# Hybrid attention step: one slot per step of a head, indexer scores in two blocks, the whole search under the projection

## The chip, the cores and the metric

The kernel runs on one core of a Trainium2 chip. A core has TensorE (PE: matrix products, its results go to the PSUM banks), VectorE (DVE), ScalarE (ACT), GpSimd (POOL) and SyncE (SP), which here only issues DMAs. Each engine runs its own instructions in the order of the program; semaphores tie the engines together. The metric is the time of one execution on the device in microseconds, lower is better.

## What is computed

One encoder layer for 1024 prompt tokens and 64 tokens of a second request that has 256 cached keys. All is float32. Cut to what matters:

```
h = rms_norm(x) * (1 + scale) + shift                      # modulated by silu(c) @ w_ada
dq,dk,dv, sq,sk,sv, iq,ik,iw = split(h @ w_in)             # 4 differential heads, 8 sparse heads, 4 indexer heads
# differential head:
a = softmax(q1 k1 + bias) - lam * softmax(q2 k2 + bias)    # keys up to the query's chunk of 64
o = rms_norm(a @ v, g_subln) * (1 - lam_init)
# sparse heads: the indexer picks min(256, L // 4) keys for each query
score = sum_h w[h] * relu(q_idx[h] . k_idx)
keep  = top_k(score)
o = softmax(q k + bias, over the kept keys) @ v
x = x + gate1 * rms_norm(concat(o) @ w_out)
x = x + gate2 * rms_norm(swiglu(h2) @ w_down)
```

The rows of dk, dv, sk, sv and ik are outputs too.

## The kernel before

The tokens form nine tiles t: eight of 128 prompt tokens, tile 8 the 64 others. Tile t sees n = 128(t+1) keys, tile 8 sees 320. The program has five parts: the modulation, the input projection in 21 blocks of 128 columns and three chunks of rows each, the attention, the output projection, and the FFN in eleven groups.

**Projection and search.** `chunk(b, c)` (L1775) makes one chunk as 24 products in three-term split precision. Between the chunks of blocks 3 to 6 stand the indexer's products, `dots(t, p)` (L1779, rows L1791): tiles 2 to 8, two heads at a time into both S banks, 14 pairs in all. ACT applies relu (L1119), DVE adds the weighted heads into `work` (L1442, L1446). A pair waits until ACT has read the pair before it. `dots_tiles` gives two tiles to each of blocks 3, 4 and 5 and tile 8 to block 6. Then DVE searches for each row's threshold: `STEPS` = 33 passes, in each of which it counts the scores above a candidate in all seven tiles (L1379) and then updates the candidates (L1397 to L1431). 28 passes run one after another beside the projection (`PROJ_STEPS`). The five others are dealt out over the first 13 slots of the attention (`LATE_PARTS`). After the passes that stand under the projection DVE makes the gates (L1460 to L1471), and PE waits for these (`gates_ready`) before it begins the attention.

**Attention.** Eight steps s for each tile, 72 in all: i = 0 to 3 are the differential heads ("dense" here, with two score maps m = 0, 1), i = 4 to 7 pairs of sparse heads (m is the head). Each engine runs a loop over slots; what an engine does in slot k belongs to several steps:

- PE, in this order: turns the first half of the weights of step k-2 (transposes, L1856), score products of step k into the banks S[0] and S[1] (L1881, plus the mask for sparse steps, L1887), turns the other half, turns the output of step k-3 (L1935), value products of step k-2 into the bank PJ[0] (L1956, L1959).
- DVE: adds the bias to map 0 of step k (L1558, which also gives the maximum), takes the reciprocals of the sums of step k-1 (L1499, L1501) and combines its two maps (L1567) or scales map 0 (L1575), adds the bias to map 1 (L1558), scales map 1 of a sparse step, reads the products of step k-2 (L1588, L1593).
- ACT: copies turned weights from the two T banks to `aT` (L1134), exponentials of step k (L1224).
- POOL: the rms of a dense head (L831, L834).
- SP: refills a ring of four bias tiles `ering` (`load_e`, L704, two DMAs for each); entry e waits until the bias of entry e-4 was added. It also loads the queries and values of the tile after next.

A dense step has one group of turned weights (8 transposes at 1024 keys), a sparse step two. The scores of step k wait until both maps of step k-1 have been read (`biased`).

At three slots near the start of each tile from 2 to 8 the ties at the threshold are settled: `compare` (DVE, slot 8t-2), turning the equal marks (PE, L1898, slot 8t-1), `ranks` (PE, L1916, into PJ[1]) and `choose` (DVE, L1525, L1529) for keys 0 to 511 in slot 8t and for the others in slot 8t+1.

Once all value products up to tile 7 are done SP loads w_out (`owraw`, L751), one block between every two bias tiles of tile 8; the output projection (L1978) starts when tile 0's split outputs are ready.

## Time and profile before

| what | us |
| --- | --- |
| median of 3 runs | 1673.65 (1671.73 to 1674.25) |
| the profiled execution | 1676.04 |
| its span in the trace | 1674.0 |
| projection, end of PE's last chunk | 382 |
| first bias of the attention | 388.5 |
| first bias of tile 2 | 459.0 |
| first bias of tile 8 | 706.1 |
| first product of the output projection | 752.0 |

The profile page gives the busy time of each engine, the span in 40 slices with TensorE's granted clock, and the chain of work that ended last. Besides, the trace answers what ran on an engine in a stretch (the timeline: start, duration, engine, line, what it wrote and read, count, and in brackets the idle time just before it with the engine that ended it), and how long each engine was busy in a stretch, with the clock granted there (1.00 is 2.4 GHz, 0.50 is 1.2 GHz). Busy times of PE count matmuls that overlap, so that a busy PE need not be one at its peak.

### The profile page before, as it was taken

Reading aid. Unit: us, or ns where it says so; the run is one execution under the profiler, and the core shown is the slowest. Engines: PE = TensorE matmul, PEld = TensorE weight load, DVE = VectorE, ACT = ScalarE, POOL = GpSimd, SP = SyncE. Lnnn points to the kernel's source line nnn. Section 1 sums busy time; section 2 is a strip of 40 time slices with the busy share of each in tenths; the row PEclk is TensorE's granted clock in tenths of the full one; section 3 lists DMA queues with packets and bytes.
Section 4 is the critical chain, followed back from the end, with each engine's and each line's share of the span. In section 5 each row is a group of like instructions: output and inputs, shape, how many; then the busy total and the mean of one; then the engine's idle time right before and its main releaser. Section 6 shows DMA issues by size and latency. Waiting matters only on the chain.

```text
span 1674.0 us, 24041 instructions
## 1 busy us (share of the span) xinstructions
PE 1535.3 (92%) x9123; PEld 1317.8 (79%) x9123; DVE 761.0 (45%) x1766; ACT 541.7 (32%) x1101; POOL 407.8 (24%) x361
## 2 busy tenths in 40 slices
PE   5999999994678889879999999999999999999996
PEld 3776998993345566648879999999999999999994
DVE  4423999996877777653430321303122031221305
ACT  4345222212466666662542112121121221112102
POOL 3010111111001000054546231332313222232315
PEclk8899999996599999969999999999999999999998
DMA  9210465522244444341442110111011021110006
GB/s 300 79 45 26 129 213 183 179 90 80 68 119 123 125 128 124 84 153 40 125 131 83 51 51 25 50 50 50 25 50 50 25 69 31 50 50 25 0 1 125
DMA packets 147336, 142.49 MB, mean 85 GB/s; under 512 B 11982, under 2 KB 129039, under 8 KB 147259
## 3 DMA queue, kind: packets, MB, share of 16 engines
q1 hardware_dynamic: 146026, 137.01, 27.9%
q0 software_dynamic: 1232, 4.46, 1.5%
q8 instruction: 48, 0.79, 0.2%
q14 instruction: 30, 0.24, 0.1%
HBM read 122.14 MB, written 19.29 MB: 84 GB/s over the span
## 4 chain that ended last, share of the span: by engine, by line
PE 82%; DVE 8%; issue 3%; ACT 3%; POOL 2%; DMA 1%; SPq 1%; DVEq 0%; POOLq 0%; ACTq 0%
PE S L2017 31%; PE PJ L1746 14%; PE T L2040 10%; PE PJ L2040 5%; PE S L1881 4%; DVE sc L1558 3%; PE S L1978 3%; PE PJ L1978 3%; PE T L1856 3%; PE PJ L1956 2%; PE S L1709 1%; DVE scrap L1379 1%; PE S L1791 1%; PE S L1887 1%; ACT aT L1134 1%
## 5 line engine op out<-in xcount | busy, mean ns | idle before, releaser
L2017 PE MATMUL S<-h2h,gh 128*128 128x352 f32 (+1 forms) x1056 | 347.9, 329 | 7.5 <-POOL gl L895 4.0
L2017 PE MATMUL S<-h2h,gl 128*128 128x352 f32 (+1 forms) x1056 | 346.7, 328 | 0.0
L2017 PE MATMUL S<-h2l,gh 128*128 128x352 f32 (+1 forms) x1056 | 346.5, 328 | 0.0
L1664 DVE TENSOR_TENSOR hv<-sg,S 128x352 f32<-128x352 f32 (+1 forms) x66 | 35.1, 532 | 490.1 <-ACT sg L1278 478.0
L2017 PEld LDWEIGHTS S<-h2h,gh 128*128 128x128 f32 x1056 | 199.6, 189 | 8.4 <-issue 7.9
L2017 PEld LDWEIGHTS S<-h2l,gh 128*128 128x128 f32 x1056 | 200.4, 190 | 0.4
L2017 PEld LDWEIGHTS S<-h2h,gl 128*128 128x128 f32 x1056 | 199.3, 189 | 0.0
L1379 DVE TENSOR_SCALAR_CACHE_REDUCE scrap<-work,cand 128x384 uint8<-128x384 f32 (+6 forms) x217 | 180.1, 884 | 1.1
L2040 PE MATMUL T<-dh,ahl 128*128 128x512 f32 x504 | 166.5, 390 | 0.0
L1746 PE MATMUL PJ<-hTh,wh 128*128 128x352 f32 (+2 forms) x480 | 161.3, 336 | 0.0
L1278 ACT ACTIVATE sg<-S 128x352 f32<-128x352 f32 (+1 forms) x66 | 31.2, 474 | 399.6 <-PE S L2017 399.6
L1746 PE MATMUL PJ<-hTl,wh 128*128 128x352 f32 (+2 forms) x480 | 158.4, 330 | 0.0
L1746 PE MATMUL PJ<-hTh,wl 128*128 128x352 f32 (+2 forms) x480 | 158.4, 330 | 0.0
L922 POOL TENSOR_TENSOR ahl<-hv,ahl 128x352 fp32r<-128x352 f32 (+1 forms) x66 | 61.0, 925 | 354.9 <-ACT ahl L1134 354.9
L1224 ACT ACTIVATE sc<-sc,nmax 128x128 f32<-128x128 f32 (+8 forms) x144 | 107.8, 749 | 84.1 <-DVE nmax L1558 83.1
L1558 DVE CUSTOM_DVE_ANT_0 sc<-S,ering 128x128 f32<-128x128 f32 (+8 forms) x144 | 104.2, 724 | 47.5 <-PE S L1881 31.1
L1671 DVE TENSOR_TENSOR yacc<-yacc,T 128x512 f32<-128x512 f32 x132 | 90.7, 688 | 75.2 <-PE T L2040 75.2
L840 POOL TENSOR_TENSOR wl<-wraw,wh 128x1024 fp32r<-128x1024 f32 (+1 forms) x21 | 49.6, 2364 | 287.6 <-ACT wh L976 287.6
L2040 PEld LDWEIGHTS T<-dh,ahl 128*128 128x128 f32 x504 | 94.6, 188 | 20.2 <-DVE yacc L1671 0.8
L1856 PE MATMUL T<-ident,sc 128*128 128x128 f32 (+2 forms) x468 | 76.7, 294 | 30.3 <-DVE sc L1567 21.1
L2040 PE MATMUL T<-dl,ahl 128*128 128x512 f32 x264 | 102.9, 390 | 0.0
L895 POOL TENSOR_TENSOR gl<-graw,gh 128x2048 fp32r<-128x2048 f32 x22 | 101.2, 4602 | 2.0 <-ACT gh L1134 2.0
(244 smaller groups left out, 2466.4 us busy)
## 6 DMA issues: line engine op xcount, KB each, us to landing
graw<-in_w_gu SPq DMA_DIRECT2D x44, 512.0 KB, 5.0
ada<-in_w_ada SPq DMA_DIRECT2D x16, 1024.0 KB, 7.4
draw<-in_w_down SPq DMA_DIRECT2D x22, 512.0 KB, 3.3
wraw<-in_w_in SPq DMA_DIRECT2D x20, 512.0 KB, 5.6
ada_first<-in_w_ada SPq DMA_DIRECT2D x8, 1024.0 KB, 12.5
q_scratch<-qst SPq DMA_DIRECT2D x8, 544.0 KB, 2.9
xin<-in_x_p SPq DMA_DIRECT2D x8, 512.0 KB, 7.0
owraw<-in_w_out SPq DMA_DIRECT2D x8, 512.0 KB, 4.9
```

The lines of the kernel that those rows point to most:

```text
L895: pool.tensor_tensor(gl[slot][:, :, :], graw[slot][:, :, :], gh[slot][:, :, :].bitcast(F32), ALU.subtract).then_inc(g_lo, 1)
L922: last = pool.tensor_tensor(al[:, slot, c0:c0 + p], hv[:, u % 2, 0:p], ah[:, slot, c0:c0 + p].bitcast(F32), ALU.subtract)
L1224: nc.scalar.activation(p, p, ACT.Exp, scale=-1.0, bias=nmax[0:r, slot % 4, m:m + 1], accum_out=rsum[0:r, slot % 4, m:m + 1]).then_inc(exp_ ...
L1379: ins = nc.vector.tensor_scalar(out, work[0:r, o:o + n], least_score, None, ALU.is_ge, ALU.add, accum_out=rows_at(count, i))
L1558: nc.vector.tensor_tensor_reduce(out=sc[0:r, s % 3, m, 0:n], in0=S[m][0:r, 0:n], in1=rev, scale=-1.0, scalar=3.0e38, op0=ALU.add, op1=ALU.min,
L1671: nc.vector.tensor_tensor(at, at, YB[u % 3][:, :], ALU.add).then_inc(y_added, 1)
L1746: last = pe.matmul(chunk_bank(3 * b + c)[0:w, 0:n], wp[:, b % 2, k, 0:w], hp[:, k, c0:c0 + n], start=(k == 0 and p == 0), stop=(k == KB - ...
L1856: last = pe.transpose(bank[0:w, 128 * j:128 * j + r], sc[0:r, s % 3, m, o:o + w], ident[0:r, 0:r])
L1881: last = pe.matmul(S[m][0:r, o:o + w], qt[part, t % 2, i, 0:r], keys, start=True, stop=not kept)
L1978: last = pe.matmul(OUT[t % 2][0:r, cols_], op[:, k, 0:r], wp[:, k, cols_], start=(k == 0 and p == 0), stop=(k == KB - 1 and p == 2))
L2017: last = pe.matmul(S[u % 2][:, 512 * part:512 * part + n], wp[slot][:, k, 128 * part:128 * part + 128], hp[:, k, c0:c0 + n], start=(k == 0 ...
L2040: last = pe.matmul(YB[u % 3][:, :], ap, wp[:, b, 512 * half:512 * half + 512], start=(b == 0 and p == 0), stop=(b == 1 and p == len(parts) ...
```

## The change

Four things change, all of them in order and buffers; no operation is added or left out.

1. `dots_pairs` puts the eight pairs of tiles 2 to 5 into block 3 and the six of tiles 6 to 8 into block 4: one before each chunk and one in the middle of each; what is left of a block's pairs follows its last chunk.
2. All 33 search passes run before the gates. `LATE_PARTS`, `late_parts` and `scrap2` go.
3. In the attention the step that an engine works on in slot k is k-1 for the exponentials, k-2 for combining or scaling (DVE), k-3 for turning the weights (PE, ACT), k-4 for the value products, k-5 for the last scaling of a dense head, and k-6 for turning its output. There are 78 slots where there were 75. `sc` gets a fourth buffer (`sc_last`), `aT` a second, and the value products use PJ[0] and PJ[1] in turn; `ranks` takes the one that the value products don't use in that slot.
4. The order within a slot becomes, on PE: value products, all transposes of weights, equal marks, output, scores, ranks; on DVE: both biases, combining or scaling, last scaling, reading of the products, compare, choose.

Two waits come with it: the value products wait until `choose` has read its bank in the slot before (`rank_read`), and `ranks` waits until the products of the step before have been read (`wait_products_read`).

PE in a slot of tile 7 with a dense step (T<-ident,sc are the transposes of weights, S<-kTp,qt the scores, T<-ident,ob the output of a head, PJ the value products). Before:

```order
L1959 MATMUL PJ<-vsbp,aT 128x128 [waits o_read,ld_v1,t_freed1,t_freed0]
L1959 MATMUL PJ<-vsbp,aT 128x128 x7
L1856 MATMUL T<-ident,sc 128x128 [waits t_freed0,combined]
L1856 MATMUL T<-ident,sc 128x128 x3
L1856 MATMUL T<-ident,sc 128x128 [waits t_freed1,combined]
L1856 MATMUL T<-ident,sc 128x128 x3
L1881 MATMUL S<-kTp,qt 128x512 [waits biased]
L1881 MATMUL S<-kTp,qt 128x512 x3
```

Now, the last dense slot of the tile:

```order
L1958 MATMUL PJ<-aT_107,vsbp 64x128 [waits t_freed1,t_freed0,pair_read]
L1958 MATMUL PJ<-aT_107,vsbp 64x128 x13
L1871 MATMUL T<-ident,sc 128x128 [waits t_freed0,combined]
L1871 MATMUL T<-ident,sc 128x128 x3
L1871 MATMUL T<-ident,sc 128x128 [waits t_freed1,combined]
L1871 MATMUL T<-ident,sc 128x128 x3
L1896 MATMUL S<-kTp,qt 128x512 [waits biased]
L1896 MATMUL S<-kTp,qt 128x512 x3
```

Read as a ring the order of these three is the same, but the weights that are turned ahead of the scores of step k were those of step k-2 and are those of step k-3. For a sparse step the second half of the transposes stood behind the scores, and now all of them stand ahead.

DVE in a dense slot of the same tile (ISA sc,nmax<-S,ering is the bias, L1567 and L1571 combine the maps). Before:

```order
L1499 RECIPROCAL rinv<-rsum 128x2 [waits exp_done]
L1501 SCALAR_TENSOR_TENSOR rlam<-rinv,lam,rsum 128x1 [waits vchain]
L1567 SCALAR_TENSOR_TENSOR sc<-sc,rlam 128x1024 [waits vchain]
L1558 ISA sc,nmax<-S,ering 128x1024 [waits ld_e3,qk_done]
L1558 ISA nmax 128x1
```

Now (the row ISA sc,nmax comes twice, with a row of its accumulator behind each):

```order
L1557 ISA sc,nmax<-S,ering 128x1024 [waits t_filled0,t_filled1,ld_e0,qk_done]
L1557 ISA nmax 128x1
L1557 ISA sc,nmax<-S,ering 128x1024 [waits ld_e1,qk_done]
L1557 ISA nmax 128x1
L1508 RECIPROCAL rinv<-rsum 128x2 [waits exp_done]
L1510 SCALAR_TENSOR_TENSOR rlam<-rinv,lam,rsum 128x1 [waits vchain]
L1571 SCALAR_TENSOR_TENSOR sc<-sc,rlam 128x1024 [waits vchain]
```

The bias of map 1 stood behind the combining and stands ahead of it now.

PE at the second slot of tile 7, where the ranks of ties are made (PJ<-upto,eqT). Before:

```order
L1956 MATMUL PJ<-aT,vsbp 64x128 [waits t_freed1,t_freed0,o_read]
L1956 MATMUL PJ<-aT,vsbp 64x128 x13
L1916 MATMUL PJ<-upto,eqT 128x512 [waits rank_read]
L1916 MATMUL PJ<-upto,eqT 128x512 x4
L1916 MATMUL PJ<-upto,eqT 128x384
L1916 MATMUL PJ<-upto,eqT 128x256
L1916 MATMUL PJ<-upto,eqT 128x128
L1856 MATMUL T<-ident,sc 128x128 [waits t_freed0,combined]
L1856 MATMUL T<-ident,sc 128x128 x3
L1856 MATMUL T<-ident,sc 128x128 [waits t_freed1,combined]
```

Now:

```order
L1931 MATMUL PJ<-upto,eqT 128x384
L1931 MATMUL PJ<-upto,eqT 128x256
L1931 MATMUL PJ<-upto,eqT 128x128
L1958 MATMUL PJ<-aT_89,vsbp 64x128 [waits t_freed0,pair_read,t_freed1,rank_read]
L1958 MATMUL PJ<-aT_89,vsbp 64x128 x13
L1871 MATMUL T<-ident,sc_last 128x128 [waits t_freed0,scaled]
L1871 MATMUL T<-ident,sc_last 128x128 x3
L1871 MATMUL T<-ident,sc_last 128x128 [waits t_freed1,scaled]
L1871 MATMUL T<-ident,sc_last 128x128 x2
L1871 MATMUL T<-ident,sc_last 128x128 [waits t_freed0,scaled]
```

The value products (PJ<-aT) follow the ranks across the slot's border and have got a wait for `rank_read`, and the transposes behind them wait with them.

The diff, cut to its core:

```diff
-PROJ_STEPS = 28
-LATE_PARTS = [(j, i) for j in range(PROJ_STEPS, STEPS) for i in range(len(TOPK_TILES) + 1)]
-LATE_POINTS = 3 * 13
-def dots_tiles(b):
-    return [t for t in TOPK_TILES if b == 3 + (t - 2) // 2]
+def dots_pairs(b, point):
+    pairs = [(t, p) for t in {3: [2, 3, 4, 5], 4: [6, 7, 8]}.get(b, []) for p in range(2)]
+    return pairs[point:point + 1] if point < 6 else pairs[6:]
...
+SCALE_LAG, TURN_LAG, VALUE_LAG, OUT_LAG = 2, 3, 4, 6
+SLOTS = NSTEPS + OUT_LAG
...
+        sc_last = place("sc_last", [128, 2, 1024], F32, 183296)
+        aT.append(then("aT1", [128, 2, 8, 128]))
...
             dve.wait_ge(targets_set, 3 * len(TOPK_TILES) + 1)
-            for j in range(PROJ_STEPS):
+            for j in range(STEPS):
...
             for slot in range(SLOTS):
                 for m in range(2):
                     if slot < NSTEPS:
+                        biases(slot, m)
+                s = behind(slot, SCALE_LAG)
+                if s is not None:
+                    weights(s)
+                s = behind(slot, VALUE_LAG + 1)
+                if s is not None and not sparse(s):
+                    head_scaled(s)
+                s = behind(slot, VALUE_LAG)
+                if s is not None and not sparse(s):
+                    head_read(s)
                 if tie_stage(slot, 0):
                     compare(tie_stage(slot, 0))
                 for q in range(2):
                     t = tie_stage(slot, 2 + q)
                     if t and 512 * q < nkeys(t):
-                        choose(t, q)
+                        choose(t, q, PJ[(slot + 1) % 2])
...
-            def chunk(b, c):
+            def chunk(b, c, between):
...
                 for k in range(KB):
+                    if k == KB // 2:
+                        for pair in between:
+                            dots(*pair)
                     chunk_rows(b, c, k)
...
+            def value_products(s):
...
+                for q in range(2):
+                    u = tie_stage(s + VALUE_LAG - 1, 2 + q)
+                    if u and 512 * q < nkeys(u):
+                        pe.wait_ge(rank_read, rank_count(u, q))
...
             for slot in range(SLOTS):
-                for key in prob_part(slot, 0):
-                    transpose_probs(key)
-                if slot < NSTEPS:
-                    scores(slot)
-                for key in prob_part(slot, 1):
-                    transpose_probs(key)
+                s = behind(slot, VALUE_LAG)
+                if s is not None:
+                    value_products(s)
+                s = behind(slot, TURN_LAG)
+                if s is not None:
+                    for key in prob_groups(s):
+                        transpose_probs(key)
                 if tie_stage(slot, 1):
                     turn_equals(tie_stage(slot, 1))
...
+                if slot < NSTEPS:
+                    scores(slot)
                 for q in range(2):
                     t = tie_stage(slot, 2 + q)
                     if t and 512 * q < nkeys(t):
-                        ranks(t, q)
+                        if slot > VALUE_LAG:
+                            wait_products_read(pe, slot - VALUE_LAG - 1)
+                        ranks(t, q, PJ[(slot + 1) % 2])
```

## Rows read from the trace of the kernel before

**Rows 1.** Busy times by stretch: start:end us, length, each engine, clock, DMA share, GB/s

```profile
388.50:459.00 70.50, 39.91 (x165) 22.20 (x167) 61.87 (x238) 25.95 (x101) 5.94 (x16) 0.53 0.31 76
459.00:706.10 247.10, 213.96 (x1627) 138.92 (x1626) 183.06 (x482) 156.80 (x367) 17.82 (x48) 1.00 0.43 119
...
652.30:667.16 14.86, 12.97 (x114) 8.56 (x114) 10.58 (x18) 9.09 (x18) 0.00 (x0) 1.00 0.41 96
667.16:692.50 25.34, 22.73 (x142) 14.98 (x143) 19.14 (x44) 14.91 (x27) 2.97 (x8) 1.00 0.39 113
692.50:706.10 13.60, 12.38 (x119) 8.72 (x118) 9.03 (x19) 9.92 (x21) 0.00 (x0) 1.00 0.18 39
706.10:752.00 45.90, 33.75 (x239) 20.00 (x239) 26.22 (x84) 28.23 (x82) 20.36 (x16) 0.67 0.45 142
```

**Rows 2.** Waits of PE from 459.0 to 706.1: us, times, longest

```profile
PE T L1856 <- DVE sc L1567: 13.8, 21, 1.1
```

**Rows 3.** Timeline of PE in tile 7: start us, us, engine, line, out<-in

```profile
670.12 1.09 PE L1856 MATMUL T<-ident,sc 128*128 128x128 f32 x8 [0.99 <-DVE sc L1567]
671.26 1.99 PE L1881 MATMUL S<-kTp,qt 64*128 64x512 f32 x8
673.18 0.33 PE L1935 MATMUL T<-ident,ob 128*128 128x128 f32 x1
673.55 2.02 PE L1959 MATMUL PJ<-vsbp,aT 128*128 128x128 f32 x16
676.22 1.09 PE L1856 MATMUL T<-ident,sc 128*128 128x128 f32 x8 [0.65 <-DVE sc L1567]
```

**Rows 4.** Timeline of DVE over the same slot, and a sparse scaling

```profile
673.28 1.23 DVE L1558 CUSTOM_DVE_ANT_0 sc<-S,ering 128x1024 f32<-128x1024 f32 x1 [0.24 <-PE S L1881]
...
674.43 0.16 DVE L1499 RECIPROCAL rinv<-rsum 128x2 f32<-128x2 f32 x1
674.62 0.22 DVE L1501 SCALAR_TENSOR_TENSOR rlam<-rinv,lam,rsum 128x1 f32<-128x1 f32 x1
674.88 1.28 DVE L1567 SCALAR_TENSOR_TENSOR sc<-sc,rlam 128x1024 f32<-128x1024 f32 x1
676.08 1.22 DVE L1558 CUSTOM_DVE_ANT_0 sc<-S,ering 128x1024 f32<-128x1024 f32 x1
...
688.00 0.75 DVE L1575 TENSOR_SCALAR sc<-sc,rinv 128x1024 f32<-128x1024 f32 x1
```

**Rows 5.** Timelines of PE and DVE in the first slot of tile 7

```profile
654.14 1.75 PE L1956 MATMUL PJ<-aT,vsbp 128*64 128x128 f32 x28 [0.94 <-ACT aT L1134]
...
656.58 0.75 DVE L1525 SCALAR_TENSOR_TENSOR eq<-PJ,need,eq 128x512 bf16<-128x512 f32 x1 [0.49 <-PE PJ L1916]
```

**Rows 6.** Timeline of the projection: two products 10 apart; the search's ends, a slow step

```profile
169.85 0.32 PE L1746 MATMUL PJ<-hTh,wl 128*128 128x352 f32 x1
171.46 0.32 PE L1746 MATMUL PJ<-hTh,wh 128*128 128x352 f32 x1
...
174.51 0.55 DVE L1379 TENSOR_SCALAR_CACHE_REDUCE scrap<-work 128x384 uint8<-128x384 f32 x1
...
304.83 2.38 POOL L840 TENSOR_TENSOR wl<-wraw,wh 128x1024 fp32r<-128x1024 f32 x1 [12.38 <-ACT wh L976]
304.88 2.35 DVE L1423 TENSOR_TENSOR good<-count,target 128x7 f32<-128x7 f32 x1
...
375.70 0.17 DVE L1428 TENSOR_SCALAR step<-step 128x7 f32<-128x7 f32 x1
```

**Rows 7.** Timelines of SP's queue and DVE: second round of bias tiles, step 4's bias

```profile
396.93 15.60 SPq L704 DMA_DIRECT2D ering<-r_scratch  x14
...
405.57 0.28 DVE L1558 CUSTOM_DVE_ANT_0 sc<-S,ering 128x128 f32<-128x128 f32 x1
```

**Rows 8.** Busy times by stretch, the columns as in rows 1

```profile
718.00:721.40 3.40, 1.85 (x12) 0.97 (x12) 2.36 (x11) 1.54 (x8) 0.73 (x2) 1.00 0.73 231
721.40:724.80 3.40, 3.40 (x14) 1.27 (x12) 2.20 (x8) 2.33 (x7) 1.46 (x3) 0.50 0.76 225
```

More of the change, by code:

```diff
@@ L142, in prob_groups, with behind @@
     return [("p", s, m, q) for m in range(2 if sparse(s) else 1) for q in range((n + 3) // 4)]
[L145 to L150 removed]
+def behind(slot, lag):
+    return slot - lag if lag <= slot < NSTEPS + lag else None
 def tie_stage(slot, lag):
@@ L184 @@
 T_ORDER += [("gates",)]
-for _s in range(NSTEPS + 3):
-    if 2 <= _s < NSTEPS + 2:
-        T_ORDER += prob_groups(_s - 2)
+for _s in range(SLOTS):
+    if behind(_s, TURN_LAG) is not None:
+        T_ORDER += prob_groups(_s - TURN_LAG)
     if tie_stage(_s, 1):
         T_ORDER += eq_groups(tie_stage(_s, 1))
-    if _s >= 3 and not sparse(_s - 3):
-        T_ORDER += [("o", _s - 3)]
+    if behind(_s, OUT_LAG) is not None and not sparse(_s - OUT_LAG):
+        T_ORDER += [("o", _s - OUT_LAG)]
 T_ORDER += [("f", t, half) for t in range(NT) for half in range(2)]
@@ L1109, in _ @@
             for b in range(NB):
-                pairs = [(t, p) for t in dots_tiles(b) for p in range(2)]
                 for c in range(4):
-                    for t, p in pairs[c:c + 1]:
+                    for t, p in dots_pairs(b, 2 * c) + dots_pairs(b, 2 * c + 1) if c < 3 else dots_pairs(b, 6):
                         r, n = rows_of(t), nkeys(t)
@@ L1208, in _ @@
             for slot in range(SLOTS):
-                if 3 <= slot < NSTEPS + 3 and sparse(slot - 3):
-                    pair_out(slot - 3)
-                for part in range(2):
-                    for key in prob_part(slot, part):
+                s = behind(slot, VALUE_LAG)
+                if s is not None and sparse(s):
+                    pair_out(s)
+                s = behind(slot, TURN_LAG)
+                if s is not None:
+                    for key in prob_groups(s):
                         prob_out(*key[1:])
@@ new lines, in weights @@
+            def weights(s):
+                _, _, r, n = step(s)
+                sums(s)
+                if sparse(s):
+                    for m in range(2):
+                        p = probs(s, m)[0:r, 0:n]
+                        nc.vector.tensor_scalar(p, p, rinv[0:r, s % 4, m:m + 1], None, ALU.mult
+                                                ).then_inc(scaled, 1)
+                else:
+                    nc.vector.scalar_tensor_tensor(out=probs(s, 0)[0:r, 0:n], in0=probs(s, 1)[0:r, 0:n],
+                                                   scalar=rlam[0:r, s % 4:s % 4 + 1], in1=probs(s, 0)[0:r, 0:n],
+                                                   op0=ALU.mult, op1=ALU.subtract).then_inc(combined, 1)
@@ L1561, in _ @@
-                    if m == 0 and 1 <= slot <= NSTEPS:
-                        sums(slot - 1)
-                    if m == 0 and 1 <= slot <= NSTEPS and not sparse(slot - 1):
-                        s = slot - 1
-                        _, _, r, n = step(s)
-                        nc.vector.scalar_tensor_tensor(out=sc[0:r, s % 3, 0, 0:n], in0=sc[0:r, s % 3, 1, 0:n],
-                                                       scalar=rlam[0:r, s % 4:s % 4 + 1], in1=sc[0:r, s % 3, 0, 0:n],
-                                                       op0=ALU.mult, op1=ALU.subtract).then_inc(combined, 1)
@@ L1597, in _ @@
-                for part in late_parts(slot, 2):
-                    search_part(*part)
+                        biases(slot, m)
[3 more added lines that the diff above has]
+                s = behind(slot, VALUE_LAG + 1)
+                if s is not None and not sparse(s):
+                    head_scaled(s)
+                s = behind(slot, VALUE_LAG)
+                if s is not None and not sparse(s):
+                    head_read(s)
@@ L1815, in _ @@
                     pe.wait_ge(chunk_out, 9)
-                pairs = [(t, p) for t in dots_tiles(b) for p in range(2)]
                 for c in range(4):
-                    for pair in pairs[c:c + 1]:
+                    for pair in dots_pairs(b, 2 * c):
                         dots(*pair)
                     if c < 3 and (b, c) not in FIRST_CHUNKS:
-                        chunk(b, c)
+                        chunk(b, c, dots_pairs(b, 2 * c + 1))
                     if c < 3 and b == 2:
@@ L1927, in _ @@
+            for slot in range(SLOTS):
+                s = behind(slot, VALUE_LAG)
+                if s is not None:
+                    value_products(s)
+                s = behind(slot, TURN_LAG)
+                if s is not None:
+                    for key in prob_groups(s):
+                        transpose_probs(key)
                 if tie_stage(slot, 1):
                     turn_equals(tie_stage(slot, 1))
-                if 3 <= slot < NSTEPS + 3 and not sparse(slot - 3):
-                    s = slot - 3
-                    r = rows_of(s // 8)
+                s = behind(slot, OUT_LAG)
+                if s is not None and not sparse(s):
+                    r = step(s)[2]
```

197 lines of the change are left out of this document (90 added, 107 removed).

## The prediction

> **What bounds the kernel now.** I read the page's 40 slices first, then the busy times by stretch, then the waits and timelines inside one tile. From 459.0 to 706.1 us (tiles 2 to 7) PE is busy 213.96 of 247.10 us at a granted clock of 1.00, DVE 183 [rows 1]: PE bounds these tiles, with 33.1 us of gaps. The largest named wait is that of the turned weights for DVE's combining, 13.8 us in 21 waits [rows 2]. The first two tiles are different: 70.5 us, PE busy 39.9 at clock 0.53, DVE 61.9, so that DVE with the late search and the supply of bias tiles set their time [rows 1]. The last 45.9 us (tile 8 and the drain) run at 0.67 [rows 1].
>
> The dense slot of tile 7 shows how the engines depend on each other. Scores start at 671.26, map 0's bias at 673.28 (2.02 later), the reciprocal 1.15 after that, then 0.19, 0.26 and 1.20 to the end of combining; the transposes start 0.14 later at 676.22, and take 1.14 up to the next scores [rows 3, 4]. The sum is 6.10 us, the slot's length (670.12 to 676.22) [rows 3]. So a dense slot is already one closed loop PE, DVE, PE, and only the bias of map 0 stands in it; map 1's bias runs beside the transposes.
>
> **The change part by part. 1, attention of tiles 2 to 7.** The larger distance between steps would open the loop if PE gave DVE the scores early. But PE still issues the scores of step k behind the transposes, now those of step k-3; DVE makes these weights in slot k-1, behind both biases of step k-1, and these need the scores of step k-1. So the loop closes over one slot again: scores, bias 0, bias 1, combining, transposes, scores. It contains all it had plus map 1's bias, 1.15: 6.10 + 1.15 = 7.25 us. Value products (2.02) don't add to it; PE has them while DVE works.
> - Slots 3 to 6 of tile 7 on PE: 7.25; with the mask products of a sparse step 7.9 twice (a slot with them takes 0.64 more now); with mask and output turning (0.37, rows 3) 8.2. Sum 31.25 instead of 25.34 [rows 1]: +5.9.
> - Slots 1 and 2, with ties. Here the value products at the head wait for `choose`, which is the last thing on DVE, and everything else of PE is queued behind them: transposes, scores, ranks; DVE waits for those scores in its turn. 2.02 (scores), 2 x 1.15 (biases), 0.2 (sums), 2 x 0.67 (scalings, row of 0.75 less overlap), 0.79 (`choose`), 1.75 (value products), 2.0 (both halves of the transposes) make 10.4, with an output 10.8 [rows 3 to 5]; with 0.4 for handovers 21.6 for both instead of 14.86 [rows 1]: +6.7. The second operation of `choose` frees no bank and is left out.
> - Slot 7 and slot 0 of the next tile: sparse scalings instead of combining, both halves of transposes, output, equal marks: 9.5 and 7.0, the latter with tile 8's small scores. 16.5 instead of 13.60 [rows 1]: +2.9.
>
> Tile 7: +15.5. If this falls with the keys (384 to 1024 in tiles 2 to 7, together 4.125 times tile 7's), it is 64 us for the six tiles; if it doesn't fall, 93. I take **+70**, near the lower end, since most terms are by element, but handovers aren't.
>
> **2, TensorE's clock.** Now PE is busy 0.87 of the time in tiles 2 to 7 and keeps 1.00 [rows 1]. In the tie slots it would idle some 5 us in one piece, in dense slots 7.25 - 5.2 = 2 us. In the tail the clock read 1.00 over 718.0 to 721.4, where PE was busy 1.85 of 3.40, and 0.50 (1.2 GHz) right after, with PE busy all the time [rows 8]. Such a stretch at half rate loses 1.7 us, two of them 3.4: I take 2.5 for a fall, and one fall at each of the 11 tie slots of tiles 2 to 8: **+28**. Bounds: 0 (no fall) and 45 (falls outside the tie slots too). The Trainium skill, "TensorE: Matmul & The Clock Gate", section "HAM oscillation", describes the same pattern: short bursts of matmuls with waits between them put the array back to half rate every time. By that rule the 28 stands, without it the sum is 28 lower.
>
> **3, first two tiles.** Five search passes leave DVE: 35 counts and 5 updates, at the projection's 7.2 us a pass (201.4 us from 174.51 to 375.87 for 28, rows 6) 33 to 36 us of its 61.9. Not all of this is won. Slots 0 to 3 use bias tiles that are loaded; SP issues the next only at 396.93, behind its loads of values [rows 7], which the change doesn't move, so step 4 can't start before about 400.6, by my estimate of landing (it starts at 405.57 now, rows 7): 4.9 won. The other twelve slots take 4.46 us each now; with two biases, combining and copies at 128 and 256 keys and PE at half clock I estimate 3.3: 14 won. Together **-19**, bounds -10 (each slot still bound by bias tile supply or PE at clock 0.53) and -30 (all of DVE's relief).
>
> **4, projection.** The 14 pairs stay, twice as dense: one every half chunk. Ten products take 1.61 us [rows 6], half a chunk (12) 1.9; a pair has to wait for ACT's two relus, about 2 us, so PE waits little inside the chunks, but three pairs stand back to back at the end of block 3. I take **+4**, 0 to 9 with a clock fall. The dots end 4.5 chunks (of 24 products, 3.9 us) earlier, with the turns of natural rows some 21 us: the search begins near 153.5. 33 passes at 7.2 end at 391, 9 us past the projection's end of 382 and 15 later than the passes now. Costed at about nothing: before 388.5 no bias starts today, and step 4 is held to 400.6 by SP anyway; without that cover it would cost 3 to 8. One row bears on the pass's length: an update's two-input operation took 2.35 us where it met POOL's subtraction of 2.38 [rows 6], while its like take 0.17. The Trainium skill, "SBUF - State Buffer", section "Who interferes with whom", has it so: an operation of VectorE with two inputs in SBUF can't run while GpSimd reads SBUF through the shared pair. The 7.2 contains these meetings, and the five added passes would meet one or two more.
>
> **5, tail.** Three more slots, and SP's wait for the last value products stands behind all bias issues. 45.9 us now [rows 1]. Each drain slot costs a turn of transposes, copies and products, about 3: **+9**, bounds 4 and 14.
>
> Costed at nothing: exponentials a slot later (ACT has 34 us of work in tile 7's 53.8, rows 1), POOL's rms, the fourth `sc` and second `aT` (no operation more), `ranks`' wait for products read a slot before. Added DMAs: none. Out-projection and FFN unchanged.
>
> **Sum.** The profiled execution took 1676.0, 2.4 over the median. 1676.0 + 70 + 28 - 19 + 4 + 9 = 1768; less 2.4 gives **1765 us**, 5.5% more.
>
> **The rivals.**
> - *A, loop without clock falls.* PE idles, but the clock stays at 1.00. For it: in 459 to 706 it never fell, though single waits of 1 us stood there; against it: rows 8. 1765 - 28 = 1737, 1718 to 1745.
> - *B, faster: the pipeline opens.* If DVE has the weights of step k-3 combined before PE reaches the transposes, PE's waits go. That is so if biases, sums and combining (2 x 1.15 + 0.45 + 1.20 = 3.95) are done while PE still has work behind the scores. For it: the step distance is one more, and PE's work for a dense slot is only 5.2. Against it: after the scores PE has only value products, 2.02, from which 3.95 decides against; it would turn at a combining under 2 us. All gaps gone: 1673.7 - 19 - 33 = 1622, about 1624 with rests.
> - *C, a smaller loop.* DVE starts bias 0 while map 1's scores still run, and value products cover more: half of the 70, no falls, and a cheap tail: 1690 to 1715.
> - *D, the change doesn't do what it says.* The search isn't all under the projection: it ends after 391, with more meetings, and the cover of part 4 is too short. +8: 1773.
>
> **How the numbers follow.** Forecast (loop and falls, 1745 to 1795) 0.52; A 0.30; B 0.08; C 0.05; D 0.03; within the measurement's reach 0.02. What a measurement of this kernel can tell from no change is about 0.2%. Faster by more than that: B, 0.08. Within: 0.02. Slower: the rest, 0.90. The range must take in A and most of C: from 1712; above, the upper ends of the loop (93 instead of 70) and clock (45 instead of 28) don't both come: 1800. Left out are B, some of C and a little above 1800.
>
> **What would show it.** The dots ending and the search beginning near 153; search ending near 388 to 391, with PE's gates right behind; first bias about 391; tile 2's at 440 to 446. In tile 7 dense slots of 7.3 to 8 us, in them PE's first transposes waiting some 2 us for the combining, and the second bias standing ahead of it; tie slots of 10 to 11 us in which the value products wait for `keep` or `eq` of DVE. Granted clock under 1.00 in slices of tiles 2 to 7 (if 1.00 stays: A). PE's waits for DVE in tiles 2 to 7 over 80 us instead of 13.8. The prediction is wrong if dense slots stay at or under 6.1, or if tiles 2 to 7 together take under 290 us.

## The result, and the profile after

The changed kernel takes 1766.09 us, median of four runs (1762.67 to 1774.72), against 1673.95 for the kernel before: the ratio is 1.056 (95% interval 1.052 to 1.060). The profiled execution took 1766.25 us, with a span of 1764.4. The times of stages that follow are those of one profiled execution each, taken at the same marks in every kernel: PE's last chunk of the projection, the first bias of a tile, the first product of the output projection, the end.

| stage | before, us | after, us | difference | forecast |
| --- | --- | --- | --- | --- |
| start to the end of the projection | 381.8 | 380.0 | -1.8 | +4 |
| to the first bias | 6.7 | 6.7 | 0.0 | 0 |
| tiles 0 and 1 | 70.5 | 55.9 | -14.6 | -19 |
| tiles 2 to 7 | 247.1 | 346.1 | +99.0 | +98 |
| tile 8 and drain, to the output projection | 45.9 | 54.3 | +8.4 | +9 |
| output projection and FFN | 922.0 | 921.4 | -0.6 | 0 |
| sum | 1674.0 | 1764.4 | +90.4 | +92 |

Nearly all of the loss is in one stage, tiles 2 to 7. (Its forecast is the +70 for the loop and the whole +28 for the clock; one of the 11 falls behind the 28, 2.5 us, belongs to tile 8's stage.) The busy times of the attention's three stretches after the change (start:end, length, each engine, granted clock, DMA share, GB/s; they answer to [rows 1]):

```profile
386.66:442.60 55.94, 39.77 (x151) 22.14 (x152) 27.18 (x143) 24.43 (x97) 6.20 (x16) 0.50 0.39 100
442.60:788.70 346.10, 245.38 (x1599) 155.61 (x1598) 180.55 (x482) 154.34 (x364) 21.33 (x48) 0.89 0.31 84
788.70:842.97 54.27, 33.39 (x281) 22.87 (x281) 29.16 (x88) 31.70 (x90) 20.28 (x16) 0.75 0.36 119
```

In tiles 2 to 7 PE's gaps have grown from 33 to 101 us, DVE's busy time is about the same (180.6 against 183.1), and the clock is 0.89 where it was 1.00. PE's busy time is 31 us longer, since a product lasts longer at the lower clock: with the clock held at 0.98 (`pe_kept_busy` below) PE is busy 210 us with the same work. PE's waits in that stretch (us in total, times, longest) say for whom; they answer to [rows 2], where the first group was 13.8 us and DVE's `eq` did not appear:

```profile
PE PJ L1958 <- DVE eq L1534: 30.3, 10, 4.2
PE T L1871 <- DVE sc L1571: 29.5, 18, 2.4
PE T L1871 <- DVE sc_last L1571: 9.5, 6, 1.9
PE T L1871 <- DVE sc L1568: 9.4, 10, 1.1
```

The first is the value products behind `choose`, the next two are transposes behind the combining of a dense step, the last is transposes behind a sparse scaling. Together they are 78.7 us, and with the smaller groups behind them, for equal marks (2.8) and one more sparse scaling (1.7), PE waits 83 us for DVE.

One dense slot of tile 7, on PE and then on DVE, answers to [rows 3] and [rows 4]. L1557 is the bias, L1571 combines, L1871 are the transposes, L1896 the scores:

```profile
737.88 1.75 PE L1958 MATMUL PJ<-aT,vsbp 128*64 128x128 f32 x28
742.07 1.09 PE L1871 MATMUL T<-ident,sc 128*128 128x128 f32 x8 [2.44 <-DVE sc L1571]
743.09 1.99 PE L1896 MATMUL S<-kTp,qt 64*128 64x512 f32 x8
745.01 2.05 PE L1961 MATMUL PJ<-vsbp,aT 128*128 128x128 f32 x16
749.19 1.09 PE L1871 MATMUL T<-ident,sc 128*128 128x128 f32 x8 [2.13 <-DVE sc L1571]
```

```profile
737.98 1.22 DVE L1557 CUSTOM_DVE_ANT_0 sc<-S,ering 128x1024 f32<-128x1024 f32 x1 [5.44 <-PE S L1896]
739.13 0.08 DVE L1557 DVE_READ_ACCUMULATOR2_ANT nmax<- 128x1 f32 x1
739.13 1.22 DVE L1557 CUSTOM_DVE_ANT_0 sc<-S,ering 128x1024 f32<-128x1024 f32 x1
...
740.27 0.16 DVE L1508 RECIPROCAL rinv<-rsum 128x2 f32<-128x2 f32 x1
740.47 0.22 DVE L1510 SCALAR_TENSOR_TENSOR rlam<-rinv,lam,rsum 128x1 f32<-128x1 f32 x1
740.73 1.29 DVE L1571 SCALAR_TENSOR_TENSOR sc<-sc,rlam 128x1024 f32<-128x1024 f32 x1
745.11 1.22 DVE L1557 CUSTOM_DVE_ANT_0 sc_last<-S,ering 128x1024 f32<-128x1024 f32 x1 [3.10 <-PE S L1896]
```

Read it as a ring. The scores end about 737.9, both biases take 2.3, sums and combining 1.75, the transposes start at 742.07, the scores at 743.09, and the next bias at 745.11. The slot is 7.13 us; it was 6.10. DVE idles 3.10 us for PE's scores, and PE idles 2.44 for DVE's combining: each waits for the other within one slot, and no engine is full.

A slot with ties, PE and DVE:

```profile
718.64 3.25 PE L1958 MATMUL PJ<-aT,vsbp 128*64 128x128 f32 x28 [4.15 <-DVE eq L1534]
721.83 1.65 PE L1871 MATMUL T<-ident,sc 128*128 128x128 f32 x7
...
731.96 1.75 PE L1958 MATMUL PJ<-aT,vsbp 128*64 128x128 f32 x28 [3.10 <-DVE eq L1534]
```

```profile
713.87 1.22 DVE L1557 CUSTOM_DVE_ANT_0 sc<-S,ering 128x1024 f32<-128x1024 f32 x1 [3.76 <-PE S L1896]
...
716.36 1.28 DVE L1568 TENSOR_SCALAR sc<-sc,rinv 128x896 f32<-128x896 f32 x2
717.56 0.28 DVE L1596 TENSOR_SCALAR ob<-ob,oss 128x128 f32<-128x128 f32 x1
717.75 0.75 DVE L1534 SCALAR_TENSOR_TENSOR eq<-PJ,need,eq 128x512 bf16<-128x512 f32 x1
```

DVE has had the scores since 713.87, but works through two biases, two scalings and a head's last scaling before `choose` reads the ranks; only then may PE's value products, transposes and scores go on. This slot took 13.5 us, the next 10.6. The first of them ran at the lower clock: the same 28 products took 3.25 us, 1.75 in the next slot. The clock around it, by stretch:

```profile
713.00:716.40 3.40, 1.49 (x8) 0.32 (x6) 2.49 (x6) 1.37 (x4) 0.00 (x0) 1.00 0.00 0
716.40:719.80 3.40, 1.16 (x12) 1.19 (x14) 2.79 (x5) 0.00 (x0) 0.00 (x0) 0.50 0.65 168
719.80:723.20 3.40, 3.40 (x27) 3.05 (x23) 0.00 (x0) 0.50 (x2) 0.00 (x0) 0.50 0.39 66
```

PE was busy for 1.49 us of the stretch, then the clock is 0.50 (1.2 GHz), and it is still so while PE works all the time again. In the next slot PE waited 3.10 us for `choose`, and the clock stayed at 1.00: the 28 products behind that wait took 1.75 us.

### The profile page after: what moved, and what is told of

Same layout as the page of the kernel before. It is cut to its first block, busy times and chain, and to the rows that moved or that the text cites. A ratio compares the mean times of both kernels' runs of the same rounds, so it can differ in the third digit from the quotient of the medians.

```text
span 1764.4 us, 24048 instructions
## 1 busy us (share of the span) xinstructions
PE 1564.3 (89%) x9123; PEld 1336.5 (76%) x9123; DVE 754.6 (43%) x1766; ACT 541.3 (31%) x1101; POOL 410.8 (23%) x361
## 4 chain that ended last, share of the span: by engine, by line
PE 79%; DVE 9%; issue 4%; ACT 4%; DMA 2%; SPq 1%; POOL 1%; POOLq 0%; DVEq 0%; ACTq 0%
PE S L2040 30%; PE PJ L1759 13%; PE T L2063 10%; PE S L1896 5%; PE PJ L2063 5%; PE T L1871 3%; PE S L2001 3%; PE PJ L2001 2%; DVE sc L1557 2%; PE PJ L1958 2%; DVE sc L1568 1%; PE S L1722 1%; ACT aT L1140 1%; DVE sc L1571 1%; PE S L1807 1%
## 5 line engine op out<-in xcount | busy, mean ns | idle before, releaser
L1557 DVE CUSTOM_DVE_ANT_0 sc<-S,ering 128x128 f32<-128x128 f32 (+8 forms) x108 | 74.7, 725 | 166.2 <-PE S L1896 103.6
L1871 PE MATMUL T<-ident,sc 128*128 128x128 f32 (+1 forms) x351 | 59.4, 308 | 64.4 <-DVE sc L1571 41.6
L847 POOL TENSOR_TENSOR wl<-wraw,wh 128x1024 fp32r<-128x1024 f32 (+1 forms) x21 | 49.5, 2356 | 286.2 <-ACT wh L983 286.2
L1140 ACT ACTIVATE aT<-T 128x512 f32<-128x512 f32 (+4 forms) x168 | 68.9, 453 | 151.4 <-PE T L1871 151.1
L838 POOL TENSOR_SCALAR oss<-oss 128x1 f32<-128x1 f32 (+1 forms) x36 | 8.5, 236 | 408.0 <-DVE oss L1587 408.0
L1871 PEld LDWEIGHTS T<-ident,sc 128*128 128x128 f32 (+1 forms) x351 | 41.7, 155 | 81.3 <-DVE sc L1571 48.0
```

What stands on the lines that cost most here:

```text
L847: pool.tensor_tensor(wl[:, b % 2, :, 0:n], wraw[:, b % 2, :, 0:n], wh[:, b % 2, :, 0:n].bitcast(F32), ALU.subtract).then_inc(w_lo, 1)
L1140: act_copy = lambda out, in_, **kw: nc.scalar.activation(out, in_, ACT.Copy, **kw)
L1557: nc.vector.tensor_tensor_reduce(out=probs(s, m)[0:r, 0:n], in0=S[m][0:r, 0:n], in1=rev, scale=-1.0, scalar=3.0e38, op0=ALU.add, op1=ALU.m ...
L1871: last = pe.transpose(bank[0:w, 128 * j:128 * j + r], probs(s, m)[0:r, o:o + w], ident[0:r, 0:r])
```

## The experiments

All times are medians, and ratios are to the kernel before. The stages, in us, come from each kernel's own trace; the last column runs from tile 8's first bias. The diffs are cut to their core, and "..." marks what is left out.

| kernel | us | ratio (95%) | tiles 0, 1 | tiles 2 to 7 | clock there | to the output projection |
| --- | --- | --- | --- | --- | --- | --- |
| before | 1673.95 | | 70.5 | 247.1 | 1.00 | 45.9 |
| changed | 1766.09 | 1.052 to 1.060 | 55.9 | 346.1 | 0.89 | 54.3 |
| before_search | 1654.66 | 0.987 to 0.991 | 49.5 | 247.1 | 1.00 | 45.9 |
| before_search_only | 1673.46 | 0.996 to 1.000 | 47.0 | 247.1 | 1.00 | 45.9 |
| weights_mid | 1732.23 | 1.032 to 1.038 | 51.6 | 313.8 | 0.92 | 54.8 |
| choose_early | 1752.08 | 1.041 to 1.049 | 55.6 | 334.4 | 0.89 | 51.5 |
| pe_kept_busy | 1748.25 | 1.042 to 1.045 | 55.8 | 325.0 | 0.98 | 56.0 |
| scores_first | 1633.88 | 0.974 to 0.977 | 44.2 | 223.4 | 1.00 | 54.7 |
| first_mid | 1663.32 | 0.992 to 0.996 | 47.0 | 249.9 | 1.00 | 55.4 |
| first_choose | 1636.54 | 0.974 to 0.980 | 44.9 | 227.7 | 0.99 | 55.7 |
| before_first_both | 1660.30 | 0.989 to 0.994 | 50.5 | 254.0 | 0.99 | 47.9 |
| halves_apart | 1625.78 | 0.967 to 0.973 | 45.1 | 211.1 | 1.00 | 58.3 |

**Is it the attention or the search?** `before_search` has only the first half of the change (parts 1 and 2 of its list).

```diff
-PROJ_STEPS = 28
+PROJ_STEPS = STEPS
...
-    return [t for t in TOPK_TILES if b == 3 + (t - 2) // 2]
+    pairs = [(t, p) for t in {3: [2, 3, 4, 5], 4: [6, 7, 8]}.get(b, []) for p in range(2)]
+    return pairs[point:point + 1] if point < 6 else pairs[6:]
...
```

> The kernel before with the first half of the change alone: indexer pairs in blocks 3 and 4, all 33 passes under the projection, attention order as before. My budget of the change has -16 us for this half (tiles 0 and 1 14.6 shorter, projection unchanged within 1), and all of the loss from the attention's order: 1655 to 1662. Rival, tiles 0 and 1 gain from the attention's order (more distance between steps) and not from DVE's relief: 1668 or more.

1654.66 us, 19 under the kernel before, at the lower edge of the expected band. Tiles 2 to 7 are at 247.1 to the tenth, so the whole loss of the change comes from its second half. Tiles 0 and 1 take 49.5 us here and 55.9 in the changed kernel: the new attention order costs 6.4 us even there.

```profile
385.80:435.30 49.50, 38.17 (x165) 21.45 (x167) 28.27 (x147) 25.46 (x101) 5.92 (x16) 0.56 0.46 108
435.30:682.40 247.10, 214.00 (x1627) 138.96 (x1628) 183.14 (x482) 156.72 (x367) 17.72 (x48) 1.00 0.44 119
```

**Do the denser indexer pairs matter?** `before_search_only` moves the passes, but leaves the pairs in blocks 3 to 6.

```diff
-PROJ_STEPS = 28
+PROJ_STEPS = STEPS
```

> The kernel before with all 33 passes ahead of the gates, and the indexer's pairs left in blocks 3 to 6. In before_search (pairs in blocks 3 and 4 as well) the search ran from 147.0 to 379.0, the projection ended at 379.1 and the first bias came at 385.8. Here the search begins near 172 to 174, so that it ends near 404 to 406, the first bias comes near 411 to 413, 20 us or more after the projection, and tiles 0 and 1 take about 50: the whole is 1672 to 1682, the gain of moving the passes used up. Rival: PE's start is not held by the gates so long, since bias tiles are late in any case: 1660 to 1668.

1673.46 us, no difference from before that a measurement can tell. The search ran from 172.9 to 407.9, and PE waited 29.0 us for the gates. Tiles 0 and 1 gain 23.4 us, but the first bias comes at 410.3 instead of 388.5. So the earlier pairs are what makes the moved passes worth something: 19 us.

```profile
PE T L1844 <- DVE lam L1471: 29.0, 1, 29.0
```

**Is the place of the scores the cause?** `scores_first` moves one call to the head of PE's slot. The weights' transposes and the value products of a slot now come behind its scores.

```diff
             for slot in range(SLOTS):
+                if slot < NSTEPS:
+                    scores(slot)
                 s = behind(slot, VALUE_LAG)
...
-                if slot < NSTEPS:
-                    scores(slot)
```

> The changed kernel with one move: PE issues the scores of a slot at its head, ahead of value products and transposes. My theory (the loop closes over one slot because the scores stand behind the transposes, which wait for DVE's combining behind both biases): the loop opens. PE's work of a dense slot of tile 7 is 2.0 + 2.0 + 1.1, so dense slots fall from 7.1 to 9.3 to 5.2 to 5.9 us, PE's waits for DVE nearly vanish, the granted clock is 1.00 in tiles 2 to 7, these take 225 to 245 us (346 in the changed kernel, 247 before), and the whole 1635 to 1660 us, faster than before. Rival 1, the loop is real but the wait of the value products for choose is the larger half: tiles 2 to 7 stay over 290, the whole over 1705. Rival 2, the greater distance itself costs (longer chains through ACT and the T banks): nothing or little comes back, over 1740.

1633.88 us, 1 under the expected band: 132 us less than the changed kernel by this one move, and 40 less than the kernel before. Tiles 2 to 7 take 223.4 us, the clock is 1.00, and dense slots of tile 7 take 5.92, 5.16, 5.55 and 5.54. Both rivals fall: the greater distance is no cost of itself, and the wait for `choose` goes with the loop (0.16 us in the last row below, a slot at the start of tile 8). PE has hardly a gap; the largest that are left are those for ACT's copies:

```profile
432.70:656.10 223.40, 202.04 (x1562) 134.71 (x1557) 181.00 (x483) 150.95 (x362) 21.34 (x48) 1.00 0.49 132
```

```profile
PE T L1982 <- ACT aT L1140: 7.4, 16, 0.7
PE T L1871 <- ACT aT L1140: 5.4, 10, 0.7
```

```profile
662.31 1.97 PE L1958 MATMUL PJ<-aT,vsbp 128*64 128x128 f32 x32 [0.16 <-DVE eq L1534]
```

**What is map 1's bias worth in the loop?** `weights_mid` leaves PE as in the changed kernel, and puts the combining back between the biases.

```diff
-                for m in range(2):
-                    if slot < NSTEPS:
-                        biases(slot, m)
+                if slot < NSTEPS:
+                    biases(slot, 0)
                 s = behind(slot, SCALE_LAG)
                 if s is not None:
                     weights(s)
+                if slot < NSTEPS:
+                    biases(slot, 1)
```

> The changed kernel with DVE's order as before: bias of map 0, combining or scaling, bias of map 1. My theory has map 1's bias as 1.15 us of the dense loop of tile 7 and nothing of the sparse one beyond that: dense slots of tile 7 fall from 7.1 to 7.7 to 6.0 to 6.6, tiles 2 to 7 from 346 to about 310, the whole to 1720 to 1740. If only the wait for choose and the clock matter, it stays over 1755. If the loop were the whole story, tiles 2 to 7 would return to 247 and the whole to about 1665.

1732.23 us, within the expectation, with tiles 2 to 7 at 313.8. The four dense slots of tile 7 are 6.10, 6.74, 6.64 and 7.17 instead of 7.13, 9.32, 7.67 and 9.94; the first three are the lengths of the kernel before to a hundredth of a microsecond. The wait for the combining halves, and the wait for `choose` stays:

```profile
PE PJ L1959 <- DVE eq L1534: 30.0, 10, 4.2
PE T L1872 <- DVE sc L1571: 16.8, 18, 1.3
```

**What does `choose` cost at the end of DVE's slot?** `choose_early` moves it behind the biases.

```diff
+                for q in range(2):
+                    t = tie_stage(slot, 2 + q)
+                    if t and 512 * q < nkeys(t):
+                        choose(t, q, PJ[(slot + 1) % 2])
                 s = behind(slot, SCALE_LAG)
                 if s is not None:
                     weights(s)
...
-                for q in range(2):
-                    t = tie_stage(slot, 2 + q)
-                    if t and 512 * q < nkeys(t):
-                        choose(t, q, PJ[(slot + 1) % 2])
```

> The changed kernel with choose moved on DVE from the end of its slot to right behind the two biases, ahead of combining or scaling. The value products wait for it at the head of PE's slot. By my theory the tie slots are one chain in which DVE's scalings (2 x 0.67 to 0.75 plus 0.2) come before choose, so that these leave the chain up to the value products: the wait of PE for eq (30.3 us in ten waits) falls to 16 to 20. But the weights turned behind the value products then come 1.4 us later and may take half of it back, so the whole is 1748 to 1760. If the wait only moves to the transposes in full, it stays within 1760 to 1770.

1752.08 us, 14 less. PE's ten waits for `eq` in tiles 2 to 7 fall from 30.3 to 17.4 us, and its waits for the scalings and combinings hardly change:

```profile
PE PJ L1958 <- DVE eq L1534: 17.4, 10, 2.6
```

**What does the clock cost?** `pe_kept_busy` gives PE transposes of the identity where it would wait. This work is additional and its results are overwritten.

```diff
+                s = behind(slot, TURN_LAG)
+                if s is not None and s >= 15 and slot < NSTEPS:
+                    bank = t_wait_free(pe, prob_groups(s)[0])
+                    held = any(tie_stage(slot, 3 + q) and 512 * q < nkeys(slot // 8) for q in range(2))
+                    for _ in range(24 if held else 8):
+                        pe.transpose(bank[:, 0:128], ident[:, :], ident[:, :])
```

> The changed kernel with added work for PE: from tile 2 on, each slot begins with 8 transposes of the identity into the free T bank (24 in the slots where the value products wait for choose), which the weights' transposes overwrite. They stand where PE waits in any case, so they keep it busy without lengthening the loop by much. My theory prices the clock falls of tiles 2 to 7 at 28 us: the granted clock there rises from 0.89 to 0.98 or more, and the time falls to 1735 to 1752. Rival, the falls cost little since PE has slack in the loop anyway: the clock rises and the time stays within 1755 to 1775. If the added work is on the path after all, the time rises by up to 96 x 1.1 us of it.

1748.25 us. The added work in tiles 2 to 7 is 38 slots of 8 transposes and 9 of 24, PE busy for 66 us (it starts two slots into tile 2, behind that tile's tie slot), and yet the kernel is 18 us faster than the one without it. Two halves of the stretch and tile 7 alone, then PE at a tie slot and at a dense one:

```profile
441.90:571.80 129.90, 111.79 (x824) 78.04 (x823) 74.07 (x240) 63.13 (x169) 10.50 (x24) 0.95 0.36 95
571.80:766.90 195.10, 164.49 (x1296) 118.39 (x1296) 106.55 (x244) 91.22 (x195) 10.83 (x24) 1.00 0.33 87
697.20:766.90 69.70, 59.36 (x466) 42.25 (x465) 38.12 (x82) 32.24 (x65) 3.15 (x8) 1.00 0.28 68
```

```profile
710.11 2.79 PE L1971 MATMUL T<-ident 128*128 128x128 f32 x24
713.37 1.75 PE L1958 MATMUL PJ<-aT,vsbp 128*64 128x128 f32 x28 [0.47 <-DVE eq L1534]
...
742.09 1.04 PE L1971 MATMUL T<-ident 128*128 128x128 f32 x8
```

The added 24 transposes fill the wait for `choose` (0.47 us of it are left), and the same value products take 1.75 us. With the clock at 1.00 tile 7 takes 69.6 us from first bias to first bias: that is the loop and the waits for `choose` without the clock. Tiles 2 to 7 fall from 346.1 to 325.0, so the clock cost 21 us at least; the rest of the loss, 325.0 - 247.1 = 78, is that of the loop and the waits for `choose`, less what the added work may have added and what the clock of 0.95 in tiles 2 to 4 still costs.

**Is the order enough, without the distance?** `before_first_both` is `before_search` with the scores at the head of PE's slot and both biases at the head of DVE's, at the old distances.

```diff
+                if slot < NSTEPS:
+                    scores(slot)
                 for key in prob_part(slot, 0):
                     transpose_probs(key)
-                if slot < NSTEPS:
-                    scores(slot)
...
+                for m in range(2):
                     if m == 0 and 1 <= slot <= NSTEPS:
                         sums(slot - 1)
```

> The kernel before with the search under the projection, and with the scores at the head of PE's slot and both biases at the head of DVE's, but with the old distances between steps (combining of k-1, transposes and value products of k-2 in one slot, one aT, three sc). It asks whether the order alone gives the gain of scores_first or whether the distance is needed. My theory: the loop through the scores opens too, but the value products of a step now follow its own transposes at once and wait for ACT's copy (0.9 us, rows 5), and DVE combines step k-1 right behind its exponentials: dense slots of tile 7 5.9 to 6.3, tiles 2 to 7 240 to 250, the whole 1645 to 1660. If order is all, tiles 2 to 7 take 223 to 230 and the whole 1630 to 1637.

1660.30 us, 6 more than `before_search`, and tiles 2 to 7 at 254.0, 4 over the top of the expected band. The value products wait for copies of the weights that were turned just before them, and outputs and second halves for free banks:

```profile
PE PJ L1958 <- ACT aT L1133: 10.2, 14, 0.9
PE T L1937 <- ACT aT L1133: 8.0, 16, 0.7
PE T L1858 <- ACT aT L1133: 7.1, 13, 0.7
```

So neither is enough: order without distance gives 254.0, distance without order 346.1, both together 223.4.

**Does DVE's order matter once the scores are first?** `first_mid` and `first_choose` are `scores_first` with DVE's order of `weights_mid` and of `choose_early`; their diffs are those shown above.

> Scores at the head of PE's slot, and DVE's order bias 0, combining or scaling, bias 1. With the scores first the scores of step k+1 wait only for the two biases of step k; combining between them puts 1.65 us into that chain: 0.24 + 1.15 + 0.45 + 1.20 + 1.15 = 4.2 after the scores against 3.1 us of PE work. Expected: dense slots of tile 7 near 6.2 instead of 5.2 to 5.9, tiles 2 to 7 near 240 to 250 instead of 223, the whole 1650 to 1662. If the place of bias 1 no longer matters once the scores are first, it stays at 1634.

> Scores at the head of PE's slot, and choose right behind the biases on DVE. In scores_first the tie slots are the longest left (7.2 and 8.1 us in tile 7 against 5.2 to 5.9). With the scores ahead, ranks end a slot late on PE and choose waits for them, so moving it ahead puts the scalings behind that wait. I expect little: 1630 to 1640, no better than scores_first. If choose at the end of DVE's slot was what held the value products, 1620 to 1630.

`first_mid` took 1663.32 us, 1 over the expected band, with tiles 2 to 7 at 249.9: the place of map 1's bias costs 26 us there, and the wait is the scores' own, for the bias of map 1:

```profile
PE S L1897 <- DVE nmax L1557: 25.9, 27, 1.5
```

So both biases first is the better order with the scores first (223.4 against 249.9) and the worse one with the scores last (346.1 against 313.8). `first_choose` gave 1636.54, the same as `scores_first` within the runs' spread; in its trace tiles 2 to 7 take 227.7 us, 4.3 more, and the projection happened to end 6.7 us earlier (375.0 against 381.8), so that it is no better at the least.

**What is left?** `halves_apart` is `scores_first` with PE's slot in the order scores, output, first half of the transposes, value products, second half. The diff shows PE's part; the turned output moves ahead of it, and ACT copies in the matching order.

```diff
                 s = behind(slot, TURN_LAG)
                 if s is not None:
-                    for key in prob_groups(s):
+                    for key in prob_groups(s)[:2]:
                         transpose_probs(key)
+                s = behind(slot, VALUE_LAG)
+                if s is not None:
+                    value_products(s)
+                s = behind(slot, TURN_LAG)
+                if s is not None:
+                    for key in prob_groups(s)[2:]:
+                        transpose_probs(key)
```

> scores_first with PE's slot in the order scores, output, first half of the transposes, value products, second half, and ACT's order to match (first copies, then the sparse output, then the rest). What is left of PE's waits in tiles 2 to 7 of scores_first is 17.8 us for ACT's copies to empty a T bank, 0.3 to 0.7 us each, between the halves and before the output. Theory: value products between the halves hide these: tiles 2 to 7 from 223 to 210 to 216, the whole 1618 to 1630, the fastest so far. Rival: the copies then wait on each other elsewhere and the gain is under 4 us.

1625.78 us, ratio 0.970, the fastest of all. Tiles 2 to 7 take 211.1 us with PE busy 201.1:

```profile
433.10:644.20 211.10, 201.12 (x1563) 134.56 (x1564) 180.66 (x482) 151.61 (x362) 21.79 (x50) 1.00 0.53 140
```

Part of the gain is given back behind tile 7 (58.3 us to the output projection instead of 54.7).

## Why the prediction was right, step by step

The forecast was 1765, the range 1712 to 1800, and the likeliest case (loop and clock falls, 1745 to 1795) came in at 1766.09. By its own steps:

- **Loop through the scores, +70.** Right in mechanism, somewhat small. The dense slots were forecast at 7.25, 7.9, 7.9 and 8.2; with the clock held up they were 7.12, 7.68, 7.67 and 8.31. The two tie slots were forecast at 21.6 together and took 22.1, the last two at 16.5 and took 16.7. Tile 7 lost 69.6 - 53.8 = 15.8 us, forecast 15.5. What was mis-sized is the way to the other tiles: I let the loss fall nearly with the keys (64 for all six), and with the clock held up it was 8.1, 7.4, 14.9, 15.7, 16.1 and 15.8 in tiles 2 to 7, thus flat from tile 4 on, 78 in all. `scores_first` and `weights_mid` show the cause, not only the sum.
- **Clock, +28.** That the clock falls held, and the measured size is 21 (346.1 against 325.0); where and how often it falls was wrong. The prediction had one fall at each tie slot and 2.5 us for each. In the changed kernel's trace the granted clock drops 14 times in tiles 2 to 7, behind a first spell at 0.50 that tile 1 leaves. Seven drops are in tie slots; two of the ten tie slots there (tile 6's first, tile 7's second) keep 1.00 after waits of 3.76 and 3.10 us, and one lies in the first spell. The other seven are outside, two of them in dense slots of tile 7, where the scores took 3.50 us and in the next slot 1.99:

```profile
750.21 3.50 PE L1896 MATMUL S<-skDp,qt 64*128 64x512 f32 x8
759.53 1.99 PE L1896 MATMUL S<-skDp,qt 64*128 64x512 f32 x8
```

  So there were more falls than forecast, and each cost less, by the difference of 21 us about 1.5; that the two errors nearly cancel is luck. The Trainium skill, "TensorE: Matmul & The Clock Gate", section "HAM oscillation", which the prediction cited, describes falls in waits for DMA, one in every round. The trace agrees as to the pattern (PE busy 1.49 of 3.40 us, then 0.50), and not as to every wait. Rival A said 1737; the kernel with the clock nearly held up, and with 66 us of added work, took 1748.
- **First two tiles, -19.** They gave 14.6. The step that failed is that I let the attention's order cost nothing there. Relief of DVE alone is worth 21.0 (`before_search`: 49.5), so the forecast for that was close, and the new order took 6.4 back. By the prediction's own terms, step 4's bias came 12.0 us after the first bias instead of 17.0, as forecast; the other twelve slots took 3.65 us each where I had estimated 3.3, and that is the term that was mis-sized.
- **Projection, +4.** The wrong sign by 6 us, half of it from elsewhere. POOL's subtraction for one block of the projection stands ahead of the pairs, a later one behind them; the two kernels, before and after:

```profile
102.87 2.38 POOL L840 TENSOR_TENSOR wl<-wraw,wh 128x1024 fp32r<-128x1024 f32 x1 [12.67 <-ACT wh L976]
183.71 2.93 POOL L840 TENSOR_TENSOR wl<-wraw,wh 128x1024 fp32r<-128x1024 f32 x1 [12.61 <-ACT wh L976]
```

```profile
100.32 2.38 POOL L847 TENSOR_TENSOR wl<-wraw,wh 128x1024 fp32r<-128x1024 f32 x1 [12.43 <-ACT wh L983]
181.77 2.40 POOL L847 TENSOR_TENSOR wl<-wraw,wh 128x1024 fp32r<-128x1024 f32 x1 [10.86 <-ACT wh L983]
```

  Between them the pairs cost 81.45 - 80.84 = 0.6 us, not 4. Ahead of them the execution was 2.55 us earlier, in a part that the change doesn't touch, and across all kernels the projection's end lies between 375.0 and 381.8. PE's wait for relu rose from 1.2 to 3.4 us, and other waits fell.
- **Search under the projection.** I had its start near 153.5 and its end near 391, 9 us past the projection. It ran from 147.7 to 380.7, and ended 0.6 us behind the projection. Two terms were mis-sized: the start came 27 us earlier than before, where I had reckoned 21, and a pass took 7.06 us, not 7.2 (4.6 us over 33 passes). The one or two added meetings with POOL did not come: each of the two kernels shows five steps of an update at 1.9 to 2.4 us under the projection. The row of 0.17 that the prediction set beside the one of 2.35 is of a one-input operation; the same two-input operation takes 0.17 as well when it meets nothing. The cover that I named was not needed. `before_search_only` shows what it would have been worth: an end at 407.9 moved the first bias by 22 us.
- **Tail, +9.** 8.4. The first load of w_out was issued 9.9 us after the tile's first bias before, and 17.7 after the change, since it waits for tile 7's last value products, which come two slots later. That the rest follows from it is argued from the two numbers; no run changed it alone. In `halves_apart` it is 22.1 and the stage 58.3.
- **Rival B (faster).** Its condition was that DVE is done before PE reaches the transposes, and that needs work for PE behind the scores. In the changed kernel there is 2.05 us of it. `scores_first` supplies 2.7 (transposes and value products), asks only for the two biases (2.3) in that time, and makes the weights a whole slot ahead of their use; it reached 1634, near the 1624 that I had given for all gaps gone.

## What to carry to other kernels

More distance between the steps of a pipeline frees nothing while one engine's order still puts the new step's first operation behind work that waits for the other engine's last. Draw the ring over one slot: which operation releases which, in the order of each engine; the slot is at least the sum round it, whatever the lags are, and the busy shares don't show it. Change the order that opens the ring first (here one call, 132 us), then judge the order on the other engine, whose best form was the opposite before and after.

## What the runs showed of the hardware

Adding work made a kernel faster: transposes that nobody reads, 8 or 24 to a slot, raised the granted clock in tiles 2 to 7 from 0.89 to 0.98 and took 18 us off. The same 28 value products took 3.25 us at the lower clock and 1.75 at the higher. Long waits alone do not tell when the clock falls: after waits of 3.76 and 3.10 us for `choose` it stayed at 1.00, after one of 4.15 it was 0.50, and it also fell in dense slots with waits of about 2 us. In tiles 0 and 1 the clock was 0.50 to 0.61 in all twelve kernels, although the late search passes are gone in all but the kernel before; why it does not rise there no run shows, and a kernel that raised it might gain in that stage too.
